# An encoder layer with 32 experts: the expert loop written out, six homes for gate/up weights, the scatter in two parts

## The reference

```python
comb = (one_hot(expert_id, N_EXPERTS) * weight[..., None]).sum(1)   # top-2 of 8 experts in the best of 4 groups
out = jnp.zeros((B * S, D), jnp.float32)
for e in range(N_EXPERTS):                                          # 32
    hg, hu = jnp.split(t @ w_gate_up[e], 2, axis=-1)                # 1024 x 512
    out = out + comb[:, e:e + 1] * ((silu(hg) * hu) @ w_down[e])    # 256 x 1024
x = layer_norm(DEEPNORM_ALPHA * x + out, ln2_g, ln2_b)
```

## Time and profile before

| | |
|---|---|
| median of 3 runs | 517.13 us (515.64 to 517.16) |
| the profiled execution | 514.3 us, its span 512.6 us |
| PE busy | 480.7 us, 94% of the span |
| DVE, ACT, POOL busy | 240.8, 192.1, 220.2 us |
| DMA | 145.10 MB, mean 283 GB/s |
| chain that ended last | PE 79%, DMA 8%, ACT 4%, DVE 4% |

### The profile page before, as it was taken

How to read it: one execution, slowest core, us unless ns; L and a number is a source line. 1 busy time by engine, 2 the same in 40 slices (tenths; PEclk the granted TensorE clock), 3 DMA queues, 4 the chain that set the end, 5 groups by cost and what they waited for, 6 DMA issues and landing times.

```text
span 512.6 us, 7907 instructions
## 1 busy us (share of the span) xinstructions
PE 480.7 (94%) x2856; PEld 343.3 (67%) x2856; DVE 240.8 (47%) x511; ACT 192.1 (37%) x412; POOL 220.2 (43%) x186
## 2 busy tenths in 40 slices
PE   8999999998999999999988999999999999999980
PEld 6999999897999988988863544444444443344420
DVE  1088999689994563522674212222221222222116
ACT  3554545669765792543442211111110111111111
POOL 3897999657666687896316011111111110011000
PEclk9999999999999999999979999999999999999996
DMA  8799885524533535459906968999999999999922
GB/s 286 258 361 357 326 284 179 166 92 149 164 128 114 178 124 166 164 172 378 392 12 247 359 259 355 419 423 421 423 423 421 421 424 421 419 423 422 421 91 84
DMA packets 26368, 145.10 MB, mean 283 GB/s; under 512 B 3040, under 2 KB 3296, under 8 KB 13792
## 3 DMA queue, kind: packets, MB, share of 16 engines
q1 hardware_dynamic: 26336, 144.67, 73.1%
HBM read 143.61 MB, written 1.05 MB: 282 GB/s over the span
## 4 chain that ended last, share of the span: by engine, by line
PE 79%; DMA 8%; ACT 4%; DVE 4%; issue 2%; POOL 1%; SPq 1%; ACTq 0%; DVEq 0%
PE bank L1428 20%; PE bank L1168 11%; PE bank L1170 11%; PE bank L1169 11%; PE bank L1447 10%; DMA slots<-in_w_gate_up 4%; DMA raw<-in_w_in 4%; PE bank L1460 3%; PE bank L1461 2%; PE bank L1254 1%; PE bank L1224 1%; PE bank L1246 1%; POOL w_lo L437 1%; ACT kT L653 1%; ACT w_hi L498 1%
## 5 line engine op out<-in xcount | busy, mean ns | idle before, releaser
L437 POOL TENSOR_TENSOR w_lo<-raw,w_hi 128x512 fp32r<-128x512 f32 x140 | 182.2, 1321 | 53.2 <-ACT w_hi L498 50.6
L1168 PE MATMUL bank<-x_hi,w_hi 128*128 128x256 f32 x400 | 116.3, 291 | 3.1 <-POOL w_lo L437 3.1
L1428 PE MATMUL bank<-slots,raw 128*64 128x512 f32 x496 | 114.2, 593 | 0.3 <-DMA slots<-in_w_gate_up 0.3
L498 ACT CAST w_hi<-raw 128x512 fp32r<-128x512 f32 x140 | 84.5, 619 | 79.6 <-PE bank L1170 68.7
L1170 PE MATMUL bank<-x_hi,w_lo 128*128 128x256 f32 x400 | 113.3, 283 | 0.0
L1169 PE MATMUL bank<-x_lo,w_hi 128*128 128x256 f32 x400 | 113.2, 283 | 0.0
L737 DVE SCALAR_TENSOR_TENSOR bank<-slots,par,bank 128x256 f32<-128x256 f32 x232 | 92.3, 480 | 0.2
L466 POOL COPY raw<-gates 128x512 f32 x28 | 19.8, 706 | 166.1 <-PE bank L1428 145.7
L1428 PEld LDWEIGHTS bank<-slots,raw 128*64 128x64 f32 x496 | 40.1, 137 | 66.0 <-issue 64.3
L1168 PEld LDWEIGHTS bank<-x_hi,w_hi 128*128 128x128 f32 x400 | 76.7, 192 | 4.6 <-POOL w_lo L437 3.0
L1169 PEld LDWEIGHTS bank<-x_lo,w_hi 128*128 128x128 f32 x400 | 76.7, 192 | 0.5 <-issue 0.2
(11 more groups left out here) (202 smaller groups left out, 587.7 us busy)
## 6 DMA issues: line engine op xcount, KB each, us to landing
slots<-in_w_gate_up SPq DMA_DIRECT2D x62, 1024.0 KB, 13.7
slots<-in_w_down SPq DMA_DIRECT2D x32, 1024.0 KB, 15.8
raw<-in_w_in SPq DMA_DIRECT2D x48, 512.0 KB, 4.3
raw<-in_w_attn SPq DMA_DIRECT2D x8, 512.0 KB, 3.3
raw<-in_w_conv SPq DMA_DIRECT2D x8, 512.0 KB, 3.3
raw<-in_w_out SPq DMA_DIRECT2D x8, 512.0 KB, 3.3
spare<-in_w_gate_up SPq DMA_DIRECT2D x2, 1024.0 KB, 14.2
gates<-in_xT SPq DMA_DIRECT2D x2, 512.0 KB, 5.3
```

What stands on the lines that cost most here:

```text
L437: nc.gpsimd.tensor_tensor(w_lo[:, n % SPLIT, m], raw[:, b % RAW, m], w_hi[:, n % SPLIT, m].bitcast(F32), ALU.subtract).then_inc(w_lo_done, 1)
L498: nc.scalar.copy(w_hi[:, n % SPLIT, m], raw[:, b % RAW, m]).then_inc(w_hi_done, 1)
L1168: mm(dst, ah, bh, start=first, stop=False, **kw)
L1428: ins = mm(gu_bank[j * WIN:(j + 1) * WIN, :], xg[u][:, k, j * WIN:(j + 1) * WIN], w, start=(k == 0), stop=(k == KT - 1))
```

## The change

- The homes of gate/up weights are six: the four slots, SPARE (the space of `a_hi`, `a_lo`) and TOKENS (the space of `x_hi`, `x_lo`, free once the gather products have read the tokens). A table `GU_HOME` gives each expert's home; from expert 10 on an expert takes the home of the one six before it. Down weights keep their four slots.
- SP's program is written out with another order: for pair p it issues gate/up of expert 2p+1, then 2p+2, each behind the `gate_up` of its home's last tenant, then waits for `down(p-2)` and issues the two down loads.
- PE's 16 pairs are written out.
- `scatter` has a column half and a list of tiles as arguments. Half 0 of pair p-1 stands ahead of `turn_h(p)`, half 1 behind it. In pair 15 only tile 0 of half 1 stands there; tile 1 follows `down(15)`, and `scattered` rises with it.
- `slot_info` multiplies in fp32r. The weights are split in a high and a low part (`weight_hi`, `weight_lo`, made once), the table has 6 columns, and ACT adds both parts with an activation of function Copy that accumulates. `build_gather` copies two parts instead of one.

The core of the diff:

```diff
+SPARE, TOKENS = SLOTS, SLOTS + 1
+GU_HOME = [0, 1, 2, 3, SPARE, 1, 0, 2, 3, TOKENS]
+GU_HOME += [(SPARE, 1, 0, 2, 3, TOKENS)[i % 6] for i in range(EXPERTS - len(GU_HOME))]
...
-            refill(1, spared=True)
-            with sp.Fori(2, EXPERTS // SLOTS) as i:
-                refill(i)
+            def refill_gate_up(e):
+                if last_tenant(e) is None:
+                    sp.wait_ge(gathered, KT)
+                else:
+                    sp.wait_ge(gu_done, last_tenant(e) // 2 + 1)
+                load_gate_up(e)
+
+            refill_gate_up(SLOTS + 1)
+            for p in range(SLOTS // 2, PAIRS):
+                if p > SLOTS // 2:
+                    refill_gate_up(2 * p + 1)
+                if p < PAIRS - 1:
+                    refill_gate_up(2 * p + 2)
+
+                sp.wait_ge(down_done, 2 * (p - 1))
+                for e in (2 * p, 2 * p + 1):
+                    load_down(e)
...
                 nc.scalar.copy(token[u], info_bank(p)[:, 0:1])
                 for j in range(2):
-                    ins = nc.scalar.copy(weight[u][j * WIN:(j + 1) * WIN, :],
-                                         info_bank(p)[j * WIN:(j + 1) * WIN, 1 + j:2 + j])
+                    rows_j = slice(j * WIN, (j + 1) * WIN)
+                    ins = nc.scalar.activation(both_parts[rows_j, :], info_bank(p)[rows_j, 1 + 2 * j:3 + 2 * j], ACT.Copy,
+                                               accum_out=weight[u][rows_j, :])
...
             for u in range(2):
-                ins = nc.vector.tensor_copy(info[u][:, :, 0:1], con[:, C_TOKEN:C_TOKEN + TT].unsqueeze(2))
+                for n in (0, 5):
+                    ins = nc.vector.tensor_copy(info[u][:, :, n:n + 1], con[:, C_TOKEN:C_TOKEN + TT].unsqueeze(2))
             chained(ins)
+            chained(nc.vector.tensor_copy(weight_hi, rt[:, 6, :, :]))
+            chained(nc.vector.tensor_tensor(weight_lo, rt[:, 6, :, :], weight_hi.bitcast(F32), ALU.subtract))
...
-                nc.vector.tensor_copy(info[u][:, :, 1:3], rt[:, 6, :, two]).then_inc(gat_built, 1)
+                for n, part in enumerate((weight_hi, weight_lo)):
+                    ins = nc.vector.tensor_copy(info_parts[u][:, :, :, n], part[:, :, two])
+                ins.then_inc(gat_built, 1)
...
-                    ins = mm(info_bank(p)[:, 0:3], gat[u][:, t, :], info[u][:, t, :], start=(t == 0), stop=(t == TT - 1))
+                    ins = mm(info_bank(p)[:, 0:6], gat[u][:, t, :], info[u][:, t, :], start=(t == 0), stop=(t == TT - 1))
...
+            def scatter(p, u, c, tiles=range(TT), first=False):
+                if c == 0:
+                    pe.wait_ge(scatter_built, p + 1)
+                pe.wait_ge(y_lo_done, 2 * p + (c + 1))
+                for t in tiles:
+                    ...
+                if c and t == TT - 1:
+                    ins.then_inc(scattered, 1)
+
+            def pair(p):
+                u = p % 2
+                if p >= 1:
+                    gate_up(p, u)
+                    if p == 1:
+                        gather_sorted()
+                        pe.wait_ge(xgT_odd, KT // 2)
+                        pe.wait_ge(xgT_even, KT // 2)
+                    scatter(p - 1, 1 - u, 0, first=(p == 1))
                 turn_h(p)
-                if not last:
+                if p >= 1 and p < PAIRS - 1:
+                    scatter(p - 1, 1 - u, 1, first=(p == 1))
+                elif p == PAIRS - 1:
+                    scatter(p - 1, 1 - u, 1, [0])
+                if p < PAIRS - 1:
                     slot_info(p + 1, 1 - u)
+                for e in (2 * p, 2 * p + 1):
+                    pe.wait_ge(wd_loaded[e % SLOTS], 16 * (e // SLOTS + 1))
                 down(p, (2 * u, 2 * u + 1))
...
+            for p in range(PAIRS):
+                pair(p)
+                if p == PAIRS // 2 - 1:
+                    pe.wait_ge(x1_set, 2 * TT)
+                    residual(first=False)
+            scatter(PAIRS - 2, 0, 1, [1])
+            for c in range(2):
+                scatter(PAIRS - 1, 1, c)
```

More of the change, by code:

```diff
@@ L380, in _ @@
             sp.wait_ge(out_done, 2 * TT)
[L381 to L383 removed]
+            load_gate_up(SLOTS)
             sp.wait_ge(load_known, 1)
@@ L1401, in slot_info, with products @@
                 for t in range(TT):
-                    ins = mm(info_bank(p)[:, 0:3], gat[u][:, t, :], info[u][:, t, :], start=(t == 0), stop=(t == TT - 1))
+                    ins = mm(info_bank(p)[:, 0:6], gat[u][:, t, :], info[u][:, t, :], start=(t == 0), stop=(t == TT - 1))
                 ins.then_inc(info_done, 1)
-            def gate_up(p, u, turn, more=False):
+            def products(p, u, weights):
                 if from_pair(p, 2):
@@ L1413, in gate_up, with weights, gate_up_more @@
                 for k in range(KT):
-                    c = k // (KT // 2)
                     if is_pair(p, 0) and k % 2 == 0:
                         pe.wait_ge(first_copied, k // 2 + 1)
+                    n = slice(k % (KT // 2) * 2 * HIDDEN, (k % (KT // 2) + 1) * 2 * HIDDEN)
                     for j in range(2):
[L1418 to L1429, removed]
-                ins.then_inc(gu_done, 1)
+                        ins = mm(gu_bank[j * WIN:(j + 1) * WIN, :], xg[u][:, k, j * WIN:(j + 1) * WIN],
+                                 weights(j, k // (KT // 2), k % (KT // 2) == 0)[:, n], start=(k == 0), stop=(k == KT - 1))
+                ins.then_inc(gu_done, 1)
+            def gate_up(p, u):
+                def weights(j, c, first):
+                    e = 2 * p + j
+                    if first:
+                        pe.wait_ge(gu_loaded[GU_HOME[e]][c], 16 * load_number(e))
+                    return gu_home(e, c)
+                products(p, u, weights)
+            def gate_up_more(n, u):
+                products(n, u, lambda j, c, first: slots[:, 0, c * GU_HALF:(c + 1) * GU_HALF])
             def turn_h(p):
@@ L1449, in down @@
                     ins.then_inc(down_done, 1)
[L1451 to L1470, removed]
+            def scatter(p, u, c, tiles=range(TT), first=False):
[3 more added lines that the diff above has]
+                for t in tiles:
+                    dst = out_bank[2 * t + c][:]
+                    s = scatter_matrix[u][:, t * P:(t + 1) * P]
+                    n = slice(c * HALF, (c + 1) * HALF)
+                    mm(dst, s, y_hi[:, n], start=first, stop=False, skip_group_check=True)
+                    ins = mm(dst, s, y_lo[:, n], start=False, stop=True, skip_group_check=True)
+                if c and t == TT - 1:
[5 more added lines that the diff above has]
+                    if p == 1:
                         gather_sorted()
@@ L1474, in pair @@
                         pe.wait_ge(xgT_even, KT // 2)
[L1475 to L1476 removed]
+                    scatter(p - 1, 1 - u, 0, first=(p == 1))
                 turn_h(p)
[L1478 removed]
+                if p >= 1 and p < PAIRS - 1:
[3 more added lines that the diff above has]
+                if p < PAIRS - 1:
                     slot_info(p + 1, 1 - u)
[L1480 to L1481 removed]
+                for e in (2 * p, 2 * p + 1):
+                    pe.wait_ge(wd_loaded[e % SLOTS], 16 * (e // SLOTS + 1))
                 down(p, (2 * u, 2 * u + 1))
             gather_first()
[L1485 removed]
+            gate_up(0, 0)
             slot_info(0, 0)
[L1487 to L1499, removed]
+            for p in range(PAIRS):
[6 more added lines that the diff above has]
+                scatter(PAIRS - 1, 1, c)
             load = pe.value_load(load_i[0:1, 0:1], min_val=0, max_val=SEQ)
@@ L1508, in _ @@
                         slot_info(n, u)
-                        gate_up(n, u, 0, more=True)
+                        gate_up_more(n, u)
                         turn_h(n)
                         down(n, (0, 0))
-                        scatter(n, u)
+                        for c in range(2):
+                            scatter(n, u, c)
 def kernel(x, w_in, b_gate, w_dw, b_dw, conv_ln_g, conv_ln_b, w_conv_proj, attn_sink, w_attn_proj, w_out,
```

50 lines of the change are left out of this document (29 added, 21 removed).

## The result

The changed kernel takes 507.73 us in the median (506.77 to 508.63, 4 runs) against 516.38 us of the kernel before (513.97 to 517.16, 4 runs), a ratio of 0.985 (0.982 to 0.989). Measured again beside 23 runs of the kernel before (515.25 us), it takes 507.66 us, ratio 0.988 (0.984 to 0.991). The profiled run took 506.77 us, its span 504.9, against 514.3 and 512.6 before: 7.7 us of span where 5.9 were forecast.

A forecast was written before the change was run, and what follows sets the result against it. PE at 13.5 us a pair and the DMA at 14.9 bound the kernel. Gaining 7.5 us and losing 1.6 in the tail gave 5.9: 508.4 profiled, 511.2 in the median with 2.8 on top; range 508.8 to 515.3.

The forecast's parts named there:

- Which limit ends last: At `down(14)`: PE alone would start it at 469.8, its weights land at 474.4, so the loads set it.
- The order on PE: Between `gate_up` and `down`: 2.5 us instead of 3.13, saving 0.6 a pair, 8.4 us in all for pairs 1 to 14.
- The copies of pair 0: In pair 0, DVE's added copies delay h by 0.5 us, with 0 and 1.1 as bounds.
- Code loads: Loading PE's written out code delays the weight loads up to down 29 by 0.4 us.
- The tail: Behind `down(15)`: the norm's statistics start 7.9 us after its start instead of 6.3, a loss of 1.6 us.
- The sum behind `gate_up(0)`: From there to the end: 7.5 us gained at `down(15)` less 1.6 in the tail, 5.9 us.
- the base and its bounds: Whole run: median before 517.1, 2.8 above the profiled run, carried over to 511.2; range 508.8 to 515.3.
- Nothing of the first half moves: Ahead of the expert part: the change to the loads moves nothing there.
- 1: PE's order saves nothing in the expert pairs: gain 2.2 us, 514.9; chance 0.12.
- 2, the clock: PE's waits in the last pairs bring 1.2 GHz for some 7 us: 3.4 us lost, 514.6; chance 0.06.
- 3: About 6 code loads in pairs 3 to 14 delay one DMA engine: down 29 lands 7.2 later, 518.0; chance 0.08.
- 4: ACT's Copy needs a table load of 1.28 us ahead of silu each pair: 524.6; chance 0.07 with other slower ones.

The follow-up runs named there:

- e1: The changed kernel again with nothing edited: 507.66 us, ratio 0.988 to the kernel before.
- e2: The changed kernel with the old order on PE, keeping the new homes and load order: 513.61 us, ratio 0.997 to the kernel before.
- e3: The changed kernel with the old homes and load order, keeping the new order on PE: 514.77 us, ratio 1.000 to the kernel before.
- e10: The changed kernel with `scatter(14)` whole ahead of `down(15)`: 507.96 us, ratio 0.986 to the kernel before.
- the two filled kernels: The kernel before and the changed kernel, each with PE's idle time in the router filled by extra products: 512.06 and 506.48 us.
- e4: The changed kernel with expert 9's gate/up issued ahead of SP's wait for `down(1)` and `scatter(14)` whole ahead of `down(15)`: 505.86 us, ratio 0.984.
- e7: The changed kernel with the slot look-up in fp32 instead of fp32r: 509.76 us, ratio 0.988 to the kernel before.
- e11: The changed kernel with expert 9's gate/up issued ahead of SP's wait for `down(1)`: 508.61 us, ratio 0.985 to the kernel before.

## Why the prediction was right, and where it was wrong

- **Which limit ends last:** right. `down(14)` waits for loads, at 472.72, 200.9 us behind `gate_up(0)`; forecast 474.4 - 273.4 = 201.0. e1 shows the waits (1.94 and 1.88 us, forecast 1 to 2), e2 and e3 either limit alone. That the time fits to 0.1 us is luck: the second down load of pair 3 landed 35.3 us behind `gate_up(0)`, 1.2 earlier than my sum has it (310.0 - 0.6 + 0.5 - 273.4 = 36.5), as the two landed 2.5 and not 3.5 us apart and the copies cost nothing, and the 66 loads from there on took 0.9 longer.
- **The order on PE:** right. `down` starts 2.5 us behind `gate_up` (forecast 2.5), 12.94 us a pair (12.9). Most of it does go into waiting for loads.
- **The copies of pair 0:** I took 0.5; h starts behind an idle 1.41 us of DVE, so it was 0. The bound below held. From DVE's timeline:

```profile
266.85 2.40 DVE L1116 CAST info<-weights 128x4 fp32r<-128x4 f32 x2
...
269.50 2.40 DVE L1116 CAST info<-weights 128x4 fp32r<-128x4 f32 x2
273.31 0.48 DVE L1141 SCALAR_TENSOR_TENSOR pT<-pT,kT,bank 128x256 f32<-128x256 f32 x1 [1.41 <-ACT pT L678]
```

- **Code loads:** I took 0.4. From the second down load of pair 3 (landed at 307.2) to down 29 (472.6) lie 165.4 us, for 66 loads of 2.487 = 164.1: 1.3 us of delay, so the term was too small. Nearly all of it lies in two landings, at 327.6 and 330.9. One of the six code loads of this stretch is beside them (326.7); the other five (352.5 to 463.8) go by with every landing within 0.1 us of its time. The kernel before loses 1.4 us at 329.0 and 332.7, beside its code load at 329.4. So the longer code did not bring this delay, and its cause stays open.
- **The tail:** right. 1.7 us lost (forecast 1.6), and e10 gets it back.
- **The sum behind `gate_up(0)`:** 239.2 - 233.0 = 6.2 us, forecast 5.9.
- **The step that failed is the base and its bounds.** I took the median as 517.1 and "2.8 above the profiled one", from three runs, and carried that difference over to 511.2. 23 runs of the same kernel put its median at 515.25, 1.0 above the profiled run, and the changed kernel's first median is also 1.0 above its profiled run (507.73 and 506.77). That is 1.9 of the 3.5 us between 511.2 and 507.7. The other 1.6 lie between the forecast of the profiled run, 508.4, and its 506.8: "Nothing of the first half moves" put what lies ahead of `gate_up(0)` at nothing, and the range's low end took in only terms behind it; but that part, which the two filled kernels show to be as fast in both, came out 1.5 us earlier in this execution. Over the executions that end lies between 271.4 and 274.4 us (270.2 with the router filled): up to 1.9 us of spread ahead of the ranks, and the router's low clock for 3.4 or 6.8 us. With 515.25 less 5.9 the forecast would have been 509.3 us, and with this spread, some 1.5 us, as a term of its own, the range would have held 507.7.
- **What stays of the difference.** 7.6 us between the medians (515.25 and 507.66) is more than the 6.2 behind `gate_up(0)`. In the means it is 7.0 (515.0 over 51 runs, 507.9 over 10). The mean granted clock was 0.983 and 0.984; from clocks and spans of the single runs I estimate that 1.2 GHz was granted for 17.4 us in the kernel before and 15.9 in the changed one, which at half speed is 0.8 us more. Why the kernel before has more of it is not shown.
- **Rivals.** 1 fell (the order does save). 2, the clock, came true in three places: in pair 0, at `down(13)`, and in e4, e7 and e11 at `down(14)`. Its price at each place is 1.7 us, not 3.4, and at `down(13)` the next wait for loads hid it. What I held against it, a wait of 1.4 us in pair 14, was a weak sign: half of the array went on for most of it, and PE was idle for 0.34 us alone. 3 fell as it was written: the six code loads are there, but five of them delay nothing, and the delay of 1.3 us is not more than before. 4 fell: no table load in the loop. Here the Trainium skill ("ScalarE: Activation LUTs", "Table sets: the hidden batching unit") named the right outcome ahead. The rule of the Trainium skill on the shared port ("SBUF — State Buffer", "Who interferes with whom") held for the copies (2.40 us for two, twice; the first pair ends where POOL's product of 2.57 us from 266.67 on does) and was of no price, as they were not last.

## What to carry to other kernels

Here PE's pace and the DMA's lay some 10% apart (13.5 and 14.9 us a pair), and a lead and a shorter loop were worth 0.3% and nothing alone, and 1.2 to 1.5% together. In such a case walk both timelines to the last weights and see which lands last. A wait of 1.9 us ahead of the last products is no longer free when it is the one that remains: look at the granted clock right behind each idle stretch, and try to fill it. Take the base of a forecast from many runs, and give what varies ahead of the change its own term.

## What the hardware showed that I had not expected

- The granted clock fell to 1.2 GHz behind idle stretches of 1.6 to 2.0 us, for 3.4 or 6.8 us, in some executions and not in others of the same code: `down(13)` took 5.35 us in one profile of the changed kernel and 3.65 in the other, behind the same idle 1.94 us. More keep-warm products in the router gave 0.6% to the kernel before (0.994, 0.992 to 0.996), nearly half of what the whole change gives.
- In a full queue the loads of 1 MiB land 2.49 us apart for over 100 us (44 loads in 109.4 us, from 363.2 to 472.6). In these traces what was lost to one late landing was not made up, and showed in all later ones.
